# The first blocks of a two-layer diffusion backbone: scales loaded in halves, x before context, three projection blocks side by side

## The reference

```python
sc  = silu(c);  scc = silu(c_ctx)[None]
mod_x = sc  @ ada_w[0] + ada_b[0]          # shifts, scales, gates for x
mod_c = scc @ ada_w[0] + ada_b[0]          # the same for context
sh1x, sc1x, g1x, sh2x, sc2x, g2x = split(mod_x, 6)
hx = rms_norm(x,  norm1_g[0]) * (1 + sc1x) + sh1x
hc = rms_norm(xc, norm1_g[0]) * (1 + sc1c) + sh1c
px = hx @ w_in;  pc = hc @ w_in            # 19 blocks of 128 columns
...                                        # gated linear attention, attention, output projection
x = x + g1x * ox
x = x + g2x * swiglu(...)                  # then layer 1 in the same way
```

## Time and profile before

| what | value |
|---|---|
| median of 3 runs | 1630.81 us (1629.42 to 1632.34) |
| the profiled execution | 1629.78 us |
| its span | 1628.0 us |
| TensorE matmul busy | 1564.7 us, 96% of the span |
| VectorE, ScalarE, GpSimd busy | 892.8, 545.3, 591.0 us |

### The profile page before, as it was taken

The page is one execution under the profiler, slowest core; times in us unless marked ns, Lnnn a source line. Parts: engine busy times, 40 slices in busy tenths (PEclk is TensorE's granted clock), DMA queues, the critical chain, the costliest instruction groups (busy, mean ns, idle before and its releaser), DMA issues.

```text
span 1628.0 us, 25137 instructions
## 1 busy us (share of the span) xinstructions
PE 1564.7 (96%) x10712; PEld 1296.0 (80%) x10712; DVE 892.8 (55%) x1250; ACT 545.3 (33%) x711; POOL 591.0 (36%) x263
## 2 busy tenths in 40 slices
PE   6999998889999999999999999999999999999997
PEld 3887763467888888888888888855568998998995
DVE  5798776668577766665566433666633221221324
ACT  5743324453422211221122243245544222232232
POOL 1273335602332322322222223345644444434442
PEclk9999999999999999999999999999999999999998
DMA  8523110034133333333433221100012222223222
GB/s 339 196 105 116 41 39 1 1 132 142 65 118 129 130 130 116 119 128 131 151 126 115 87 78 65 65 27 1 1 52 91 91 92 101 92 92 103 92 93 102
DMA packets 41631, 158.61 MB, mean 97 GB/s; under 512 B 4624, under 2 KB 5008, under 8 KB 39728
## 3 DMA queue, kind: packets, MB, share of 16 engines
q1 hardware_dynamic: 41232, 156.74, 27.4%
q0 software_dynamic: 288, 0.26, 0.1%
HBM read 154.89 MB, written 2.10 MB: 96 GB/s over the span
## 4 chain that ended last, share of the span: by engine, by line
PE 72%; DVE 3%; issue 2%; ACT 1%; POOL 0%; DVEq 0%; POOLq 0%
PE psum L1705 64%; PE psum L1905 2%; PE psum L1875 1%; PE psum L1892 1%; PE psum L1808 1%; PE psum L1877 0%; PE psum L1879 0%; PE psum L1881 0%; PE psum L1819 0%; DVE product L1063 0%; PE psum L1920 0%; DVE mxr L1209 0%; DVE xT L1536 0%; POOL acc L590 0%; PE psum L1758 0%
## 5 line engine op out<-in xcount | busy, mean ns | idle before, releaser
L1705 PE MATMUL psum<-act,whi 128*128 128x258 f32 (+2 forms) x4000 | 791.8, 318 | 6.7 <-DVE xT L1536 4.5
L616 POOL TENSOR_TENSOR wlo<-raw,whi 128x1024 fp32r<-128x1024 f32 (+1 forms) x181 | 443.4, 2450 | 916.1 <-ACT whi L647 916.1
L1705 PEld LDWEIGHTS psum<-act,whi 128*128 128x128 f32 x4000 | 592.9, 189 | 67.0 <-issue 12.1
L1705 PE MATMUL psum<-act,wlo 128*128 128x512 f32 (+1 forms) x2000 | 476.3, 317 | 0.0
L1063 DVE SCALAR_TENSOR_TENSOR product<-adr,cb 128x1024 f32<-128x1024 f32 x128 | 282.2, 2237 | 133.6 <-DMA adr<-adat_dram 128.2
L1705 PEld LDWEIGHTS psum<-act,wlo 128*128 128x128 f32 x2000 | 311.5, 189 | 27.3
L647 ACT ACTIVATE whi<-raw 128x1024 fp32r<-128x1024 f32 (+1 forms) x181 | 188.1, 1039 | 326.0 <-DMA raw<-weights_dram 325.7
L1111 DVE SCALAR_TENSOR_TENSOR tmps<-psum,rs 128x256 f32<-128x256 f32 (+1 forms) x176 | 78.0, 485 | 201.0 <-PE psum L1705 196.6
L1705 PE MATMUL psum<-gh,wlo 128*128 128x512 f32 (+1 forms) x528 | 160.9, 359 | 0.0
L1705 PE MATMUL psum<-gh,whi 128*128 128x512 f32 (+1 forms) x528 | 160.9, 358 | 0.0
L1705 PE MATMUL psum<-gl,whi 128*128 128x512 f32 (+1 forms) x528 | 159.4, 355 | 0.0
(11 more groups left out here) (182 smaller groups left out, 1235.3 us busy)
## 6 DMA issues: line engine op xcount, KB each, us to landing
raw<-weights_dram SPq DMA_DIRECT2D x181, 512.0 KB, 3.5
adr<-adat_dram SPq DMA_DIRECT2D x80, 512.0 KB, 4.4
ada_w<-ada_dram SPq DMA_DIRECT2D x8, 1024.0 KB, 15.0
xT<-x_in_dram SPq DMA_DIRECT2D x4, 1536.0 KB, 13.0
cb<-crow_dram SPq DMA_DIRECT2D x2, 1024.0 KB, 8.3
out_dram<-big SPq DMA_DIRECT2D x8, 256.0 KB, 2.2
con<-consts_dram SPq DMA_DIRECT2D x1, 512.0 KB, 7.4
con<-consts_dram SPq DMA_DIRECT2D x1, 320.0 KB, 3.1
```

The costliest lines, as they stand in the source:

```text
L616: nc.gpsimd.tensor_tensor(wlo[:, s, 0:w], raw[:, s, 0:w], whi[:, s, 0:w].bitcast(F32), ALU.subtract).then_inc(sem("s_lo"), 1)
L1705: last = MM(out_[:, o:o + t1 - t0], w_, a_[:, t0:t1], start=k == order[0] and j == 0, stop=k == order[-1] and j == 2)
```

## The change

In the queue of loads, two halves of the scales (`ada` 0 and 1, the first quarter) come first, then weight blocks 0 and 1, then the x tokens of tiles 0 to 3 alone, weight block 2, the second quarter, the x tokens of tiles 4 to 7, and last the context tokens of all tiles. The scales are made for tiles 0 to 3 from quarter 0 and for tiles 4 to 7 from quarter 1. Blocks 0, 1 and 2 are multiplied side by side, each in its own PSUM area (block 2 takes `wk[1]`, and the work on the scales moves wholly into `wk[0]`): x tokens of tiles 0 to 3, then of 4 to 7, then context and shifts. The low parts of these three weight blocks move from GpSimd to VectorE. The logits move from behind blocks 2 and 3 to behind blocks 3 and 4, the logarithms by one block too, and `decays` and `references` move behind the output of their block. Line numbers in the diff's new lines are those of the kernel after; each function keeps its name.

```diff
@@ sync
-            for h in range(ADA_RING):
-                load_ada(h)
+            load_ada(0)
+            load_ada(1)
             load_raw(0)
-            sp.dma_start(xT[:, 0:half, :], x_tiles[:, 0:half, :]).then_inc(sem("s_xa"), 16)
-            sp.dma_start(xT[:, half:KT, :], x_tiles[:, half:KT, :]).then_inc(sem("s_xb"), 16)
             load_raw(1)
+            sp.dma_start(xT[:, 0:half, 0:NX], x_tiles[:, 0:half, 0:NX]).then_inc(sem("s_xa"), 16)
+            load_raw(2)
+            load_ada(2)
+            load_ada(3)
+            sp.dma_start(xT[:, half:KT, 0:NX], x_tiles[:, half:KT, 0:NX]).then_inc(sem("s_xb"), 16)
+            sp.dma_start(xT[:, :, NX:T], x_tiles[:, :, NX:T]).then_inc(sem("s_xc"), 16)
             for h in range(ADA_RING, 2 * len(ADA_EARLY)):
                 load_ada(h)
-            load_raw(2)
@@ gpsimd
-                pool.wait_ge(sem("s_hi"), n + 1)
-                nc.gpsimd.tensor_tensor(wlo[:, s, 0:w], raw[:, s, 0:w], whi[:, s, 0:w].bitcast(F32),
-                                        ALU.subtract).then_inc(sem("s_lo"), 1)
+                if n >= RING:
+                    pool.wait_ge(sem("s_hi"), n + 1)
+                    nc.gpsimd.tensor_tensor(wlo[:, s, 0:w], raw[:, s, 0:w], whi[:, s, 0:w].bitcast(F32),
+                                            ALU.subtract).then_inc(sem("s_lo"), 1)
@@ scalar
             ada_copy(0)
-            ada_copy(1)
             high(0)
-            act.wait_ge(sem("s_modA"), 1)
+            high(1)
             for k in range(KT):
                 if k % 4 == 0:
+                    act.wait_ge(sem("s_modA"), 2 if k else 1)
                     act.wait_ge(sem("s_xb" if k else "s_xa"), 16)
                 A(act_tile("proj", 0, k, 0)[:, 0:NX], xT[:, k, 0:NX], ACT.Copy, scale=modA[:, 0, k, 0:1]) \
                     .then_inc(sem("s_nhx"), 1)
-            high(1)
+                if k == 3:
+                    high(2)
+                    ada_copy(1)
+            act.wait_ge(sem("s_xc"), 16)
...
             for k in range(KT):
-                if k == 2:
+                if k == 1:
                     ada_copy(2)
+                if k == 5:
+                    ada_copy(3)
+                if k == 6:
+                    act.wait_ge(sem("s_mod"), 4)
+                    shifts_high(NORM[0]).then_inc(sem("s_shift"), 1)
                 square(0, k, T)
-            ada_copy(3)
-            act.wait_ge(sem("s_mod"), 4)
-            shifts_high(NORM[0]).then_inc(sem("s_shift"), 1)
             root(0, T)
...
-                high(n + 2)
+                if n >= 1:
+                    high(n + 2)
@@ vector
+            def first_low(n):
+                dve.wait_ge(sem("s_hi"), n + 1)
+                TT(wlo[:, n, :], raw[:, n, :], whi[:, n, :].bitcast(F32), ALU.subtract).then_inc(sem("s_lo"), 1)
+            for h in range(2):
+                ada_reduce(h)
+                dve.wait_ge(sem("s_mod"), h + 1)
+                mod_scale(0, 4 * h, 4 * h + 4)
+                if h == 0:
+                    first_low(0)
+                    first_low(1)
...
+                if h == 0:
+                    first_low(2)
...
                 if k == 1:
+                    ada_reduce(2)
                     dve.wait_ge(*nq("sq", 0, 1))
+                if k == 4:
+                    ada_reduce(3)
+                if k == 5:
+                    dve.wait_ge(sem("s_shift"), 1)
+                    shifts_low(NORM[0]).then_inc(sem("s_shift"), 1)
                 add_square(0, k, T)
-            for c in range(2, 4):
-                ada_reduce(c)
-            dve.wait_ge(sem("s_shift"), 1)
-            shifts_low(NORM[0]).then_inc(sem("s_shift"), 1)
...
-                if n == 2:
+                if n == 3:
                     low_rank_low()
@@ tensor
-            def first_blocks(n, part):
+            def first_blocks(n, part, tiles=range(KT)):
...
+                    if n == 0 and part and k == 4:
+                        mean_square(0, T)
...
             ada_mm(0)
+            ada_T(0)
+            first_blocks(0, 0, range(0, 4))
+            first_blocks(1, 0, range(0, 4))
             ada_mm(1)
-            ada_T(0)
+            first_blocks(2, 0, range(0, 2))
             ada_T(1)
-            first_blocks(0, 0)
+            first_blocks(2, 0, range(2, 4))
+            first_blocks(0, 0, range(4, 8))
+            first_blocks(1, 0, range(4, 8))
             ada_mm(2)
-            first_blocks(1, 0)
+            first_blocks(2, 0, range(4, 6))
+            ada_T(2)
+            first_blocks(2, 0, range(6, 8))
             ada_mm(3)
-            ada_T(2)
             ada_T(3)
-            mean_square(0, T)
-            first_blocks(0, 1)
-            first_blocks(1, 1)
+            for n in range(3):
+                first_blocks(n, 1)
...
-                if n in (2, 3):
-                    logits(2 * n - 4)
-                    logits(2 * n - 3)
+                if n in (3, 4):
+                    logits(2 * n - 6)
+                    if n == 3:
+                        pe.wait_ge(*ev(2))
+                    logits(2 * n - 5)
```

More of the change, by code:

```diff
@@ L1071, in late_bias, with mod_scale @@
                     .then_inc(sem("s_mod"), 1)
-            def mod_scale(a):
+            def mod_scale(a, k0=0, k1=KT):
                 layer, second = divmod(a, 2)
                 c0 = 32 if second else 8
-                gain = par[:, PC_N + KT * a:PC_N + KT * a + KT].unsqueeze(2).to_broadcast([P, KT, 2])
-                STT(out=modA[:, a, :, :], in0=mod[:, layer, c0:c0 + KT, :], scalar=1.0, in1=gain, op0=ALU.add,
+                gain = par[:, PC_N + KT * a + k0:PC_N + KT * a + k1].unsqueeze(2).to_broadcast([P, k1 - k0, 2])
+                STT(out=modA[:, a, k0:k1, :], in0=mod[:, layer, c0 + k0:c0 + k1, :], scalar=1.0, in1=gain, op0=ALU.add,
                     op1=ALU.mult).then_inc(sem("s_modA"), 1)
@@ L1114, in _ @@
             dve.wait_ge(sem("s_par"), 16)
-            for c in range(2):
-                ada_reduce(c)
-            dve.wait_ge(sem("s_mod"), 2)
-            mod_scale(0)
-            dve.wait_ge(sem("s_modA"), 1)
-            for k in range(KT):
-                hi, lo = [act_tile("proj", 0, k, low) for low in range(2)]
-                dve.wait_ge(sem("s_nhx"), k + 1)
-                STT(out=lo[:, 0:NX], in0=xT[:, k, 0:NX], scalar=modA[:, 0, k, 0:1], in1=hi[:, 0:NX].bitcast(F32),
-                    op0=ALU.mult, op1=ALU.subtract).then_inc(sem("s_nlx"), 1)
+            def first_low(n):
[8 more added lines that the diff above has]
+                    first_low(1)
+                dve.wait_ge(sem("s_modA"), h + 1)
+                for k in range(4 * h, 4 * h + 4):
+                    hi, lo = [act_tile("proj", 0, k, low) for low in range(2)]
+                    dve.wait_ge(sem("s_nhx"), k + 1)
+                    STT(out=lo[:, 0:NX], in0=xT[:, k, 0:NX], scalar=modA[:, 0, k, 0:1], in1=hi[:, 0:NX].bitcast(F32),
+                        op0=ALU.mult, op1=ALU.subtract).then_inc(sem("s_nlx"), 1)
+                if h == 0:
+                    first_low(2)
             for k in range(KT):
@@ L1392, in linear_scan_inputs @@
             def linear_scan_inputs(n):
-                if n == 2:
+                if n == 3:
                     low_rank_low()
-                if n in (5, 6):
-                    for i in (2 * n - 10, 2 * n - 9):
-                        decays(i)
-                    for i in (2 * n - 10, 2 * n - 9):
-                        references(i)
                 if n in (7, 8):
@@ L1588, in _ @@
                             late_modulation(i)
+                    if n in (5, 6):
+                        for i in (2 * n - 10, 2 * n - 9):
+                            decays(i)
+                        for i in (2 * n - 10, 2 * n - 9):
+                            references(i)
                 if kind == "proj" and L == 1:
@@ L1649, in ada_mm @@
                     for g in range(4):
-                        last = MM(wk[0][32 * g:32 * g + 32, 512 * (c % 2):512 * (c % 2) + 512],
+                        last = MM(wk[0][32 * g:32 * g + 32, 0:512],
                                   cpad[:, 4 * half + g, :], ada_w[:, h % ADA_RING, g, :], start=half == 0,
@@ L1717, in first_blocks @@
                     pe.wait_ge(sem("s_shift"), 2)
-                for k in range(KT):
+                for k in tiles:
                     if n == 0:
@@ L2156, in _ @@
                     first_outputs(n)
-                elif n >= 2 and n != FIRST[("out", 0)] + 1:
+                elif n >= 3 and n != FIRST[("out", 0)] + 1:
                     block_products(n)
```

38 lines of the change are left out of this document (20 added, 18 removed).

## The result

The changed kernel took 1646.21 us (median of 4 runs, 1641.74 to 1648.99) against 1630.6 us before: a ratio of 1.0096, 95% interval 1.0082 to 1.011. It is slower by about 1%. The profiled execution took 1641.74 us, which is 12.0 us above the profiled one of before, and it is the fastest of the four.

What follows compares the result with a forecast made beforehand. TensorE, busy 1564.7 of 1628.0 us, was taken as the bound, so block 5's delay reaches the end: 1628.0 + 1.78 + 9.5 = 1639.3 profiled, median 1640.3. Its own range was 1638 to 1643, the whole 1634 to 1648.

Steps and rivals of the forecast that it cites:

- first product: Start of block 0 on TensorE: at 18.2 us against 22.14 before, 3.9 earlier.
- waits up to block 2's end: TensorE waits 1.0 for modA's second half, 0.7 for a copy, 1.8 for shifts, 1.65 for squares.
- block 2's end: End of the first three blocks on TensorE: at 60.95 us against 57.46 before, +3.5.
- wait ahead of block 3, its start: Block 3 waits 3.0 us for GpSimd's low part behind the root's chain, and starts at 63.95.
- wait ahead of the logits, their start: Logits behind block 3 wait 4.0 us for low_rank_low, queued on VectorE behind six late products.
- block 5's start against before: Block 5 starts on TensorE at 86.35 us against 76.86, +9.5.
- The start: First products on TensorE: clock again at the half level for 5.9 us from 18.2.
- The clock term: TensorE's clock at the half level only at the start; no cost in the new waits behind block 2.
- rival 1: Clock falls in a new gap ahead of block 3 or the logits, costing 2.95: +12.5, 1643.3 us; chance 0.22.
- One collision: A GpSimd low part delays one of VectorE's six late products, which take 9.06 us; without it 6.9, sum +7.3.
- Downstream: Behind block 5, the ends of decays moving later: costed at nothing, with 2.4 us either way as bounds.
- The median: Whole kernel: median of the runs 1.03 us above the profiled execution's forecast of 1639.3, so 1640.3.

Runs made afterwards that it cites:

- a_quarters: Changed kernel with the third and fourth quarters of the scales multiplied earlier on TensorE; 1639.23 us, ratio 1.0050 to the kernel before.
- a_lowrank: Changed kernel with low_rank_low, the low part for the logits, back ahead of block 2's output; 1641.0 us, ratio 1.0062 to the kernel before.
- b_split: Kernel before with only the loads of x cut into smaller, reordered pieces; 1628.71 us, ratio 0.9994 to the kernel before.
- a_first: Changed kernel with VectorE's low part of weight block 1 moved behind the low tiles 0 to 3; 1641.74 us, ratio 1.0070 to the kernel before.
- a_decays: Changed kernel with decays and references back ahead of the outputs of blocks 5 and 6; 1644.62 us, ratio 1.0079 to the kernel before.
- a_both: Changed kernel with the third and fourth scale quarters earlier and low_rank_low ahead of block 2's output; 1638.03 us, ratio 1.0044 to the kernel before.
- B: The kernel before the change, timed again in every series of follow-up runs; 1630.91 us beside the repeat.
- b_fill: Kernel before with 17 products that nobody reads in TensorE's 4.45 us wait ahead of the first block; 1630.73 us, ratio 1.0002 to it.
- b_apart: Kernel before with the loads of x cut and GpSimd's low part of block 0 held back until modA is made; 1628.17 us, ratio 0.9992.
- the repeat: Changed kernel timed once more without an edit, beside the kernel before; 1644.8 us, ratio 1.0081.

## Why the prediction was right, and where its sizes were off

| step | forecast | profile after |
|---|---|---|
| first product | 18.2 | 18.05 |
| waits up to block 2's end | 1.0, 0.7, 1.8, 1.65 | 1.01, 0.72, 1.51, 1.53 |
| block 2's end | 60.95 | 60.15 |
| wait ahead of block 3, its start | 3.0, 63.95 | 3.42, 63.57 |
| wait ahead of the logits, their start | 4.0, 76.45 | 2.52, 76.35 |
| blocks 3 and 4 beyond 8.5 each | 0 | 1.7 and 1.5 |
| block 5's start against before | +9.5 | +11.0 |
| span against before | +9.5 | +12.0 |

*The direction and the mechanism.* Slower was right, for the reason given. The squares and shifts wait for quarters of the scales that TensorE takes up late (a_quarters: 3.2 less in the trace, 5.6 by the medians), block 3 waits for a low part at the end of a chain from the root (it moved with the root in a_quarters), and the logits wait for a low part behind six late products (the wait went in a_lowrank). That cutting the loads of x costs nothing held: b_split; that they bind nowhere held with one exception, 0.84 us of ScalarE's time ahead of the first tile, which showed once VectorE was out of the way (a_first). The x tokens of tiles 0 to 3, forecast at 15.2, reached ScalarE at 15.84 in the changed kernel too, hidden there by VectorE's two low parts. The moved scans cost nothing that a_decays could give back.

*The start.* I took the half level for 5.9 us, as before. By the length of the steps it ended near 22.9, after some 4.8, which is worth about 0.5 us (an estimate: half of the 1.1 by which the half level was shorter). With that, a start 0.15 sooner and waits that sum to 4.8 instead of 5.15, block 2 ended 0.8 sooner than forecast.

*The clock term was mis-sized.* The sum had nothing for the clock in the new waits, and rival 1 had one fall of 2.95 us, for a wait of 4.0. Both waits brought a fall, at 3.42 and even at 2.52 us, and they cost 1.7 and 1.5. The fall in block 3 was paid out of the logits' wait (4.0 forecast, 2.52 measured, with the logits' start to 0.1 as forecast), as I had said of such a case; the one in block 4 was paid in full. That makes block 5 11.0 late instead of 9.5. Rival 1's +12.5 was nearer to the +12.0 between the profiled executions than the forecast's +9.5. The Trainium skill, TensorE: Matmul & The Clock Gate, "HAM oscillation — how this bites in real kernels", describes waits behind which TensorE starts again at the half level. The trace agrees for these two, 3.42 and 2.52 us with 0.50 granted behind each; a_both's wait of 3.41, with 1.00 granted behind it, does not. For the start of B the gain from a kept level was mostly eaten by the next waits, 0.30 and 0.59 (b_fill).

*One collision* of VectorE and GpSimd was in the sum, and was in the trace: 3.42 us. The Trainium skill, SBUF — State Buffer, "Who interferes with whom", says that a VectorE instruction with two inputs in SBUF contends with a GpSimd instruction that reads there, and that the port pair which the two share is held exclusively. b_apart agrees on both sides, 0.18 for `mod_scale` without overlap, and a first product 0.7 behind GpSimd's end. The prediction calls the product that lasted 3.41 before the fourth of six; by its start, 60.95, it was the third, which changes no sum. In the changed kernel it is the fourth, at 68.83.

*Downstream* I had nothing, bounded by 2.4 either way. TensorE's waits between 88 and 215 us sum to 7.5; before they were 5.8, the largest of them in the earlier trace rows, with 0.6 more at 86. Between 150 and 160 us the granted clock is 0.83, where it was 1.00. So the first of the 128 small products for the attention's states comes 13.1 later. The line before, then the line after:

```profile
176.56 1.48 PE L1846 MATMUL psum<-vgt,kgt 64*32 64x64 f32 x128
```

```profile
189.67 1.48 PE L1878 MATMUL psum<-vgt,kgt 64*32 64x64 f32 x128
```

That is 2.1 more than at block 5, within the bound. At the end it is +12.0, but the stretch behind that product varies by up to 6 us from execution to execution, so the 1.1 between them says nothing of the change.

*The median* moved further than the profile: 15.6 in the first comparison, 13.9 in the repeat, against 12.0 between the two profiled executions. So the other step that missed is the one that put the forecast of the median at the profiled execution's sum plus 1.03. The changed kernel's profiled execution had the highest mean clock of its four, 0.991; the others, at 0.984 to 0.987, took 3.5 to 7.3 us more. Whether the new waits make such executions more frequent is open: the repeat beside B showed no wider spread.

## What to carry to other kernels

Starting the critical engine sooner is worth what the next thing in line is late by, and here that was the norm's root. Before, it was there at 45.37, 12.1 us before TensorE had finished block 2; with three blocks in step it was there at 54.77, 5.4 us before that point, and the chain from the root to block 3 needs 8.8. When work is reordered at the start, follow what the moved result releases, queue by queue, until old and new order do the same thing again; four short waits and two long ones, with 2.64 us of work on the scales that used to lie ahead of the first product, weighed more than 4 us of earlier start. And a wait of 2.5 us on TensorE should be priced with the slower block behind it, unless another late engine swallows that too.

## What was not expected of the hardware

- TensorE's granted clock fell to the half level behind a wait of 2.52 us (at 76 to 78 us), and in a_quarters block 3 ran some 6 us at it, behind 3.40; in a_both a wait of 3.41 ahead of the same block brought no fall (1.00 from 60 to 82 us). The same wait may cost or not.
- The level was lost behind a wait of about 2 us further on too: in the changed kernel's windows it is 0.89 from 1080 to 1090 us, around a wait of 1.91 that ended at 1086.89.
- Executions of one kernel differ by some 8 us with their mean granted clock: B from 1625.97 us at 0.994 to 1633.91 at 0.989.
- At the start the windows print a granted clock of 1.00 while TensorE runs at the half level: in the changed kernel up to 22.9 us, where eight products for the scales took 1.94 us, as long as sixteen later on, and the first steps 1.28, where later ones take 0.70. The length of an instruction told the level, the window didn't.
